# A hybrid encoder's merge taken branch by branch, its branch products as three products of high and low parts, its weights through one ring of four-block units

## The reference

```python
gates = sigmoid(u @ w_in[l][:, gate columns]).reshape(bsz, t_len, 3, 1024)
proj  = stack of three products: y_s @ w_branch[l, s]      # s = 0, 1, 2; 512 -> 1024
mixed = jnp.sum(gates * proj, axis=2) @ w_out[l]           # 1024 -> 1024
h = h + _rms_norm(mixed, g[3])
```

## Time and profile before

| | |
|---|---|
| median of 3 runs | 3790.17 us (3788.57 to 3792.16) |
| the profiled execution: its time, its span | 3792.09 us, 3790.4 us |
| mean granted PE clock | 0.959 of full speed |
| PE busy, of the span | 3536.4 us, 93% |
| DVE, ACT, POOL busy | 1459.7, 1129.5, 1148.0 us |
| merge of layer 1, first matmul to last output tile done | 1253.67 to 1485.38 us |
| PE idle ahead of it, layer 1 and layer 2 | 10.93 us, 12.26 us |

### The profile page before, as it was taken

The page is one execution under the profiler, slowest core; times in us unless marked ns, Lnnn a source line. Parts: engine busy times, 40 slices in busy tenths (PEclk is TensorE's granted clock), DMA queues, the critical chain, the costliest instruction groups (busy, mean ns, idle before and its releaser), DMA issues. The chain is left out here.

```text
span 3790.4 us, 79640 instructions
## 1 busy us (share of the span) xinstructions
PE 3536.4 (93%) x32526; PEld 3310.6 (87%) x32526; DVE 1459.7 (39%) x2531; ACT 1129.5 (30%) x2113; POOL 1148.0 (30%) x852
## 2 busy tenths in 40 slices
PE   8999998888879899999999999988898789999998
PEld 7999998776768899999999999977776679999997
DVE  5331334445763214432053303534557521253312
ACT  2222352113553113222232223411145521132221
POOL 3444334110011222444344443521100212234442
PEclk9999999998998899999999999999989889999998
DMA  2333221001110322333233332200021113223332
GB/s 85 89 91 91 63 70 43 3 3 51 40 32 20 91 76 62 89 89 90 72 87 89 89 92 64 67 21 3 13 54 32 45 34 84 62 77 89 91 88 69
DMA packets 463378, 236.95 MB, mean 63 GB/s; under 512 B 19669, under 2 KB 461418, under 8 KB 463098
## 3 DMA queue, kind: packets, MB, share of 16 engines
q1 hardware_dynamic: 463098, 232.99, 22.2%
HBM read 230.57 MB, written 2.10 MB: 61 GB/s over the span
## 5 line engine op out<-in xcount | busy, mean ns | idle before, releaser
L541 POOL TENSOR_TENSOR W_low<-W,W_high 128x512 fp32r<-128x512 f32 (+1 forms) x544 | 721.0, 1327 | 908.2 <-ACT W_high L614 908.2
L141 PE MATMUL PS<-u_high,W_high 128*128 128x264 f32 x3328 | 955.2, 287 | 32.7 <-POOL W_low L718 23.2
L142 PE MATMUL PS<-u_low,W_high 128*128 128x264 f32 x3328 | 944.7, 284 | 0.0
L143 PE MATMUL PS<-u_high,W_low 128*128 128x264 f32 x3328 | 944.4, 284 | 0.0
L141 PEld LDWEIGHTS PS<-u_high,W_high 128*128 128x128 f32 x3328 | 628.6, 189 | 38.3 <-POOL W_low L718 23.4
L614 ACT ACTIVATE W_high<-W 128x512 fp32r<-128x512 f32 (+1 forms) x544 | 335.6, 619 | 1005.4 <-PE PS L143 966.7
L142 PEld LDWEIGHTS PS<-u_low,W_high 128*128 128x128 f32 x3328 | 629.1, 189 | 1.2
L143 PEld LDWEIGHTS PS<-u_high,W_low 128*128 128x128 f32 x3328 | 625.9, 188 | 0.0
L141 PE MATMUL PS<-u_high,dW_high 128*128 128x264 f32 (+1 forms) x1536 | 466.5, 304 | 15.4 <-POOL dW_low L1530 8.0
L1530 POOL TENSOR_TENSOR dW_low<-dW,dW_high 128x512 fp32r<-128x512 f32 x128 | 208.7, 1638 | 850.5 <-ACT dW_high L1525 850.3
L142 PE MATMUL PS<-u_low,dW_high 128*128 128x264 f32 (+1 forms) x1536 | 443.2, 289 | 0.0
(11 more groups left out here) (345 smaller groups left out, 5309.8 us busy)
## 6 DMA issues: line engine op xcount, KB each, us to landing
W<-in_ffn_w_in SPq DMA_DIRECT2D x352, 256.0 KB, 2.9
dW<-in_w_in SPq DMA_DIRECT2D x188, 256.0 KB, 2.9
W<-in_ffn_w_out SPq DMA_DIRECT2D x160, 256.0 KB, 2.9
W<-in_w_in SPq DMA_DIRECT2D x32, 512.0 KB, 5.8
W_branch<-in_w_branch SPq DMA_DIRECT2D x16, 768.0 KB, 5.1
W<-in_w_out SPq DMA_DIRECT2D x16, 512.0 KB, 4.2
W<-in_ffn_w_out SPq DMA_DIRECT2D x32, 128.0 KB, 2.3
xt<-in_x SPq DMA_DIRECT2D x4, 512.0 KB
```

Source lines behind the costliest of these rows:

```text
L141: nc.tensor.matmul(dst, wh, xh, start=first, stop=False)
L142: nc.tensor.matmul(dst, wh, xl, start=False, stop=False)
L143: return nc.tensor.matmul(dst, wl, xh, start=False, stop=final)
L541: g.tensor_tensor(WL[:, r, 0:nk], W[:, r, 0:nk], WH[:, r, 0:nk].bitcast(F32), ALU.subtract).then_inc(S("split"), 1)
```

## The change

The three branches are taken one after the other. All weights of the merge go through one ring of `R = 4` slots of four blocks (128x512, 256 KB), in the order of a list `units`: eight branch tiles of branch 0 (one unit each), then for s = 1, 2 and each `m` a gate tile (two units) and a branch tile (one unit), then eight output tiles (two units each), 72 units in all. A branch product is made with `exact`, from `yh` and `yl`: ACT copies the four rows of `y_of[s]` to float32r (`y_high`), DVE subtracts (`y_low`), once for each branch, with one buffer for all three. The mixture is added up in `gates[:, m]` itself, so that `acc` goes, and `WB` with it. Output tile 0 is no longer left open: PE waits for the mixture of m = 7 ahead of its last block.

```diff
-            acc = sb(st, "acc", [P, 2, T])
+            R = 4
+            W, WH, WL = (sb(st, n, [P, R, 4, P], dt) for n, dt in (("W", F32), ("W_high", F32R), ("W_low", F32R)))
+            yh = sb(st, "y_high", [P, 4, T], F32R)
+            yl = sb(st, "y_low", [P, 4, T], F32R)
...
-            W, WH, WL = weight_buffers(st, KD)
-            WB = sb(st, "W_branch", [P, 2, 3 * BW // P, P])
...
+            units = [("b", 0, m, 0) for m in range(KD)]
+            for s in (1, 2):
+                for m in range(KD):
+                    units += [("g", s, m, 0), ("g", s, m, 4), ("b", s, m, 0)]
+            units += [("o", 0, m, k0) for m in range(KD) for k0 in (0, 4)]
+            NU = len(units)
+            at_unit = {u: i for i, u in enumerate(units)}
...
+                    for u, (kind, s, m, k0) in enumerate(units):
+                        if u >= R:
+                            sp.wait_ge(S("split"), u - R + 1)
...
+                        sp.dma_start(W[:, u % R], src).then_inc(landed[u % R], 16)
...
+                    for u in range(NU):
+                        g.wait_ge(S("high"), u + 1)
+                        g.tensor_tensor(WL[:, u % R], W[:, u % R], WH[:, u % R].bitcast(F32), ALU.subtract
                                         ).then_inc(S("split"), 1)
...
+                    def high(u):
+                        act.wait_ge(landed[u % R], 16 * (u // R) + 16)
+                        if u >= R:
+                            act.wait_ge(done, u - R + 1)
+                        nc.scalar.activation(WH[:, u % R], W[:, u % R], ACT.Copy).then_inc(S("high"), 1)
+
+                    def y_high(s):
+                        if s:
+                            act.wait_ge(done, at_unit["b", s - 1, KD - 1, 0] + 1)
+                        for k in range(4):
+                            nc.scalar.activation(yh[:, k], y_of[s][:, k], ACT.Copy).then_inc(S("y_high"), 1)
...
+                    y_high(0)
+                    for u in range(NU + R):
+                        if u < NU:
+                            high(u)
+                        if u < KD:
+                            nc.scalar.activation(gates[:, u], gates[:, u], ACT.Sigmoid).then_inc(S("first_gate"), 1)
+                        if u < R:
+                            continue
+                        kind, s, m, k0 = units[u - R]
+                        if kind == "g" and k0:
+                            gate((s - 1) * KD + m)
+                        if kind == "b" and m == KD - 1 and s < 2:
+                            y_high(s + 1)
+                        if kind == "o" and k0:
+                            out.put(act, m, u - R + 1)
...
-                                    last = nc.tensor.matmul(branch_ps(q)[:, a], WB[:, m % 2, 4 * s + k],
-                                                            y_of[s][:, k, a * H2:(a + 1) * H2],
-                                                            start=k == 0, stop=k == 3)
...
+                        for j in range(4):
+                            if kind == "b" and m == 0:
+                                pe.wait_ge(S("y_low"), 4 * s + j + 1)
+                            if kind == "o" and m == 0:
+                                pe.wait_ge(S("mixture"), k0 + j + 1)
+                            for a in range(2):
+                                half = slice(a * H2, (a + 1) * H2)
+                                last = exact(dst[:, a], WH[:, u % R, j], WL[:, u % R, j], high_[:, x + j, half],
+                                             low_[:, x + j, half], x + j == 0, x + j == nk - 1)
+                        last.then_inc(done, 1)
...
+                    def y_low(s):
+                        for k in range(4):
+                            v.wait_ge(S("y_high"), 4 * s + k + 1)
+                            tt(yl[:, k], y_of[s][:, k], yh[:, k].bitcast(F32), ALU.subtract).then_inc(S("y_low"), 1)
...
+                        tt(halves(gates[:, m]), branch_ps(m), halves(gates[:, m]), ALU.mult).then_inc(S("multiplied"), 1)
+                    for s in (1, 2):
+                        y_low(s)
+                        for m in range(KD):
+                            n, q = (s - 1) * KD + m, s * KD + m
+                            x = gates[:, m]
```

More of the change, by code:

```diff
@@ L693, in phase_merge @@
             NG = 2 * KD
-            NT = NG + KD
-            out = Out(st, gain, 1.0, tile_done)
+            done = S("unit_done")
+            out = Out(st, gain, 1.0, done)
             with nc.Block() as block:
@@ L698, in _ @@
                 def _(sp):
[L699 to L712, removed]
+                    for u, (kind, s, m, k0) in enumerate(units):
+                        if u >= R:
+                            sp.wait_ge(S("split"), u - R + 1)
+                        src = (wb[:, 4 * s:4 * s + 4, m * P:(m + 1) * P] if kind == "b" else
+                               wo[:, k0:k0 + 4, m * P:(m + 1) * P] if kind == "o" else
+                               wv[:, k0:k0 + 4, C_GATE + s * D_MODEL + m * P:C_GATE + s * D_MODEL + (m + 1) * P])
+                        sp.dma_start(W[:, u % R], src).then_inc(landed[u % R], 16)
                 @block.gpsimd
                 def _(g):
-                    for n in range(NT):
-                        g.wait_ge(S("high"), n + 1)
-                        g.tensor_tensor(WL[:, n % 2], W[:, n % 2], WH[:, n % 2].bitcast(F32), ALU.subtract
+                    for u in range(NU):
+                        g.wait_ge(S("high"), u + 1)
+                        g.tensor_tensor(WL[:, u % R], W[:, u % R], WH[:, u % R].bitcast(F32), ALU.subtract
                                         ).then_inc(S("split"), 1)
@@ L747, in _ @@
                 @block.tensor
                 def _(pe):
[L749 to L752, removed]
-                                pe.wait_ge(act_evac, n - 1)
[L754 to L762, removed]
+                    for u, (kind, s, m, k0) in enumerate(units):
+                        pe.wait_ge(S("split"), u + 1)
+                        n, q = (s - 1) * KD + m, s * KD + m
+                        if kind == "g":
+                            if k0 == 0 and n >= 2:
+                                pe.wait_ge(act_evac, n - 1)
+                            dst, x, high_, low_, nk = gate_ps(n), k0, uh, ul, KD
+                        elif kind == "b":
@@ L772, in out_block @@
[L772 to L785, removed]
-                        else:
[L787 to L794, removed]
-                        if m:
-                            out_block(m, KD - 1)
@@ new lines, in _ @@
+                            dst, x, high_, low_, nk = branch_ps(q), 0, yh, yl, 4
+                        else:
+                            if k0 == 0:
+                                if m < 2:
+                                    pe.wait_ge(act_evac, NG - 1 + m)
+                                elif m < 4:
+                                    pe.wait_ge(S("multiplied"), 3 * KD - 3 + m)
+                                else:
+                                    pe.wait_ge(S("out_put"), m - 3)
+                            dst, x, high_, low_, nk = PS[:, 2 * (m % 4):2 * (m % 4) + 2, 0:H2], k0, mh, ml, KD
```

31 lines of the change are left out of this document (11 added, 20 removed).

## The result

In the first job (runs made together on one chip) the median went from 3791.16 us (four runs, 3788.57 to 3796.83) to 3734.66 us (four runs, 3733.39 to 3742.94): ratio 0.9852, 95% interval 0.9835 to 0.9869. The forecast was 3743, its range 3736 to 3756. The direction held; the median lies 1.3 us under the range and 8.3 under the forecast. Later jobs gave the same changed kernel medians of 3752.35 and 3747.77, so the first question is how much of the 56.5 us is the change's at all.

A forecast was written before the change was run, and what follows sets the result against it. The prediction took PE's queue of matmuls plus its gaps as the bound. Savings of 31.7 + 9.6 + 6.0 = 47.3 us from a median of 3790.2 gave 3742.9, called 3743 us, range 3736 to 3756.

The forecast's parts named there:

- Part 1: In the merges, 24 float32 branch matmuls per step become 72 float32r ones, saving 31.7 us over both layers.
- Part 2: PE's stall ahead of output tile 2 and the clock's fall behind it go, saving 9.6 us over both layers.
- Part 3: At each merge's start, a smaller first load lets PE begin sooner: 6.0 us for both layers, ends 0 and 8.5.
- Part 4: In the merges, the new work on ACT, DVE and POOL stays covered and costs nothing; 2.4 us kept for the range.
- this part's end: Upper end for the merge starts: 8.5 us saved, 2.9 us in each layer.
- I take 3.6, near the upper, since that one too is a stage's first: Layer 1 merge start: the first 256 KB load lands in 3.6 us, between bounds of 2.9 and 3.7.
- by the same share it becomes 4.5: Layer 2 merge start: the first load's 6.3 us becomes 4.5, so PE starts 3.2 us sooner.
- the lower bound: Merge start: the first load lands no faster than 2.9 us, the median of such loads.
- worst phase: At changes of branch and the last mixture, DVE held up beside POOL makes PE wait, 2.4 us for both layers.
- stall at a change of branch: Rival: late `y_low` stalls PE at four changes of branch, taking 19.2 us back, 3762 us; chance 0.07.
- bound by the stream: Rival: the merge's weight loads become the limit and the kernel is slower, 3801 us at 3.3 us per unit; chance 0.03.
- that execution lay 1.9 us above the median of the runs shown: Whole kernel: the profiled 3792.1 us was taken as 1.9 above the median, giving a base of 3790.2 us.

The follow-up runs named there:

- the undoing: The changed kernel with one float32 matmul per block for the branch products, in the new order and ring: 3780.43 us median, ratio 0.9956.
- the first-unit experiment: The changed kernel with the merge's first unit loaded from the input projection's gate columns instead of the branch weights, same size: 3744.98 us, one run.

## Why the prediction was right or wrong

**Part 1, the branch products: right.** Forecast 31.7 us. A branch tile costs 2.90 instead of 3.56, shown by the undoing, which put 3.56 back in the new ring: 24 tiles, 15.8 a layer, 31.7 for both. The stages agree: between the kernel before with tile 0 closed and the changed one lie 227.49 - 211.10 us a layer, 15.7 when the slow steps at the start (2.65 and 1.99) are taken off both, 31.5 for both.

**Part 2, the stall: right.** Forecast 9.6; closing the tile alone in the kernel before gave 8.1, and 9.4 without the slow steps of the start. The stall and the fall of the clock behind it are gone from the trace. One size in the working was off: a matmul at half clock costs 0.10 us more (0.22 instead of 0.12), not 0.121, so that the start's 2.3 us were 2.02 on average, with 1.5 to 2.9 from execution to execution.

The two together were to shorten the time from first matmul to last tile from 231.7 to 211.1. Measured: 231.56 (mean of four) to 211.1 (mean of six, 210.61 to 212.00).

**Part 3, the start: the mechanism right, the term mis-sized.** Forecast 6.0, measured 8.8: PE begins 4.85 us behind the issue (4.61 to 4.97) where it was 9.23 (8.57, 8.60, 9.85, 9.91). That is over the 8.5 that the prediction gave as this part's end. The step that failed is "I take 3.6, near the upper, since that one too is a stage's first", and "by the same share it becomes 4.5" in layer 2. The first load landed in 2.5 to 2.85, below even the 2.9 that was to be the lower bound, in both layers alike. In layer 1 PE began 4.9 us behind the issue, not 5.8; in layer 2 4.8, not 6.7. The row that I leaned on was a load from another matrix, and that is 0.6 us of the difference in each layer, by the first-unit experiment. In layer 2 the share is wrong on top of it: the 512 KB took 1.3 us longer there than in layer 1, and 256 KB from the same matrix took only 0.1 longer (3.50 and 3.39), some 1.2 us. The other 0.3 in layer 1 stays open, and so does why only the large load is slower in layer 2. The queue behind the first load is not the cause.

**Part 4, the covers: right.** The busiest unit, both changes of branch and the last mixture cost PE nothing. Operations of DVE and POOL take turns as in the earlier trace rows: the add of 1.82 us above began at 1305.41, just behind a subtract of POOL, and ended 0.55 us behind it:

```profile
1305.39 1.29 POOL L717 TENSOR_TENSOR W_low<-W,W_high 128x512 fp32r<-128x512 f32 x1 [1.62 <-ACT W_high L726]
```

The last mixture is ready 1.4 us ahead of its need. Timeline of DVE behind the last branch tile, layer 1, after:

```profile
1409.10 0.71 DVE L815 TENSOR_TENSOR part<-PS,gt 128x528 f32<-128x528 f32 x1 [5.08 <-PE PS L138]
1409.84 0.71 DVE L818 TENSOR_TENSOR gates<-gates,part 128x528 f32<-128x528 f32 x1
1410.58 1.41 DVE L820 CAST mixed_high<-gates 128x528 fp32r<-128x528 f32 x1
1412.02 0.71 DVE L821 TENSOR_TENSOR mixed_low<-gates,mixed_high 128x528 fp32r<-128x528 f32 x1
```

The turns took 1.0 us of the 2.3 to spare, in the cast. So the 2.4 us that the prediction kept for its worst phase were not lost. The Trainium skill, "SBUF — State Buffer", section "SBUF: two separate sides", has these turns, instruction by instruction, and the trace agrees (1.82 us for an add of 0.71); the wait of PE for them is not there.

**The rivals.** No stall at a change of branch; no bound by the stream: the DMA queue served 72 units at 2.90 us, and only with two slots did PE wait, 0.43 us at most, for a unit whose load came late. Smaller loads than the 1 MiB that the Trainium skill, "DMA: Bandwidth & Descriptors", section "Bandwidth", asks for cost PE nothing here: with four slots it never waited behind the start.

**Why the median fell out of the range.** With the 49.7 of the stages the forecast would have been 3740.5, inside the range. The other 5.8 us come from the step "that execution lay 1.9 us above the median of the runs shown, so the median becomes 3790.2 - 47.3": it took three runs for the kernel's time, and the range had some 2 us for where the clock rises. In the three later jobs before's median is 3794.3 to 3795.8, with runs from 3781 to 3805, and the changed kernel's 14 runs of all jobs go from 3733.18 to 3756.68, their mean 3744.9 and their median 3747.5. The RWKV stage's 10 us and the pair's 5, in each layer, are where this spread sits. The first job's runs were on the low side of it in both kernels, the changed one's more. That the median fell under the range was chance in this sense, and the later jobs' medians (3752.35 and 3747.77) lie inside it by chance too, since the base was some 5 us low (before's median over the 53 runs of all jobs is 3795.3) and Part 3 too small by 2.8. The gain itself is 49.7 by the stages and about 48 by the medians of all runs.

## What to carry to other kernels

Judge a change to one stage by that stage's length in several profiles, cut at marks that both kernels have: here it repeated within 1.5 us, while runs of one kernel lay up to 24 us apart. A float32 matmul is worth replacing by three float32r ones where both parts can be made under PE's cover (0.36 us for 0.445 here). In a chain of load, copy and subtract the size of the first unit is paid at the stage's start: 256 KB instead of 512 KB brought PE's first matmul forward by 4.4 us a layer, some 0.6 of it through the other matrix, and cost nothing behind it. Units smaller than that were not tried. A tile left open to dodge a wait holds its buffers: ask which weight waits for it.

## What the runs showed of the hardware that was not expected

PE's granted clock takes different courses at the same instructions. From 20 to 30 us behind the start of RWKV it was 1.00 in thirteen of eighteen stages; in the other five it stood at 0.50, for some 20 us, while the rows show PE busy for 3.00 of 3 us, and the stage was 7 to 11 us longer for it. Ahead of these sums PE paused for 0.23 to 1.37 us in all eighteen, and the length of the pause doesn't tell the two apart. At the start of a merge, behind a wait of 7 to 12 us, 13 to 28 matmuls ran at 0.22 us before the clock rose. A stall of 2.9 us in the output tiles was followed by a fall (0.57 over the next 4 us) in both layers; one of 0.43 us was not. And 24 records of dummy matmuls in the wait ahead of a stage had the clock up when the real ones came.
